# Prompt attention: values with high and low halves side by side, scores three units ahead, more homes for the shares

## What is computed

```python
s_c = einsum('bqghd,bcgd->bghqc', q, kc) * ATTN_SCALE          # compressed keys
p_c = masked_softmax(s_c, c_end[None, :] <= q_pos[:, None])
o_c = einsum('bghqc,bcgd->bqghd', p_c, vc)
s_s = einsum('bqghd,bgqkd->bghqk', q, k_sel) * ATTN_SCALE      # selected blocks: all blocks up to the query here
p_s = masked_softmax(s_s, (s_pos <= q_pos[...]))
o_s = einsum('bghqk,bgqkd->bqghd', p_s, v_sel)
s_w = einsum('bqghd,bwgd->bghqw', q, kw) * ATTN_SCALE          # the window
p_w = masked_softmax(s_w, ...)
o_w = einsum('bghqw,bwgd->bqghd', p_w, vw)
return g[..., 0:1] * o_c + g[..., 1:2] * o_s + g[..., 2:3] * o_w
```

## Time and profile before

| | |
|---|---|
| median of 3 runs | 1760.28 us (1758.5 to 1761.78) |
| the profiled execution | 1756.2 us, span of the trace 1754.6 us |
| mean granted TensorE clock | 0.959 |
| PE, weight loads, DVE, ACT, POOL busy over the span | 93%, 90%, 57%, 41%, 17% |
| prompt attention in the trace | about 186 to 385 us |

### The profile page before, as it was taken

The page is one execution under the profiler, slowest core; times in us unless marked ns, Lnnn a source line. Parts: engine busy times, 40 slices in busy tenths (PEclk is TensorE's granted clock), DMA queues, the critical chain, the costliest instruction groups (busy, mean ns, idle before and its releaser), DMA issues. The chain is left out here.

```text
span 1754.6 us, 31439 instructions
## 1 busy us (share of the span) xinstructions
PE 1630.3 (93%) x12602; PEld 1585.8 (90%) x12602; DVE 998.3 (57%) x1551; ACT 716.6 (41%) x1308; POOL 303.0 (17%) x758
## 2 busy tenths in 40 slices
PE   8998898987998999999998998799899999999986
PEld 8997777866998999999998998799899999999985
DVE  3344476764786435535557595758753454355562
ACT  4444475862444324313334346434442342233341
POOL 4610242440032102102200000001320121021000
PEclk9999699997999999999999999899899999999998
DMA  7744000033212222222231222131222222222211
GB/s 259 134 137 150 1 1 1 1 116 127 74 60 86 89 79 95 86 85 85 86 104 58 90 74 84 54 117 61 73 85 91 78 97 85 85 85 99 81 61 64
DMA packets 39947, 148.01 MB, mean 84 GB/s; under 512 B 6305, under 2 KB 6321, under 8 KB 39361
## 3 DMA queue, kind: packets, MB, share of 16 engines
q1 hardware_dynamic: 33264, 121.26, 21.3%
q0 software_dynamic: 6544, 24.81, 4.2%
HBM read 140.57 MB, written 9.10 MB: 85 GB/s over the span
## 5 line engine op out<-in xcount | busy, mean ns | idle before, releaser
L1805 PE MATMUL PS<-XH,HI 128*128 128x272 f32 (+1 forms) x1936 | 412.4, 295 | 40.7 <-DVE XL L1089 14.1
L1805 PE MATMUL PS<-XH,LO 128*128 128x272 f32 (+1 forms) x1936 | 405.5, 291 | 0.0
L1805 PE MATMUL PS<-XL,HI 128*128 128x272 f32 (+1 forms) x1936 | 404.9, 291 | 0.0
L1805 PEld LDWEIGHTS PS<-XH,HI 128*128 128x128 f32 x1936 | 311.3, 192 | 44.7 <-DVE LO L448 23.4
L442 ACT ACTIVATE HI<-RAW 128x1024 fp32r<-128x1024 f32 x223 | 235.4, 1057 | 283.0 <-PE PS L1805 259.0
L1805 PE MATMUL PS<-GH,HI 128*128 128x272 f32 (+1 forms) x1504 | 320.1, 295 | 23.2 <-DVE LO L448 8.3
L448 DVE TENSOR_TENSOR LO<-RAW,HI 128x1024 fp32r<-128x1024 f32 x223 | 272.3, 1222 | 102.3 <-ACT HI L442 97.0
L1805 PE MATMUL PS<-GH,LO 128*128 128x272 f32 (+1 forms) x1504 | 315.0, 291 | 0.0
L1805 PE MATMUL PS<-GL,HI 128*128 128x272 f32 (+1 forms) x1504 | 314.2, 290 | 0.0
L1805 PEld LDWEIGHTS PS<-XL,HI 128*128 128x128 f32 x1936 | 309.9, 191 | 0.1
L1805 PEld LDWEIGHTS PS<-XH,LO 128*128 128x128 f32 x1936 | 307.9, 191 | 0.0
(11 more groups left out here) (359 smaller groups left out, 1962.6 us busy)
## 6 DMA issues: line engine op xcount, KB each, us to landing
RAW<-in_w_stream SPq DMA_DIRECT2D x223, 512.0 KB, 3.3
ARENA<-in_cache_cmp POOLq DMA_DIRECT2D x32, 128.0 KB, 3.0
out_win_old<-in_win_copy POOLq DMA_DIRECT2D x1, 4064.0 KB, 19.2
X<-in_x SPq DMA_DIRECT2D x4, 544.0 KB, 7.1
X<-in_x POOLq DMA_DIRECT2D x1, 2176.0 KB, 9.2
out_y<-X POOLq DMA_DIRECT2D x1, 2176.0 KB, 6.9
ARENA<-in_cache_sel POOLq DMA_DIRECT2D x16, 128.0 KB, 2.9
ARENA<-in_cache_win POOLq DMA_DIRECT2D x4, 512.0 KB, 5.3
```

The source lines that it names most:

```text
L1805: ins = mm(PS[0:rows, b + h, 0:width], w[:, 0:rows], cols(x, x0 + n, h), start=first, stop=last)
```

## The change

It has four parts.

1. **Values in two passes.** The values' high and low halves of one head group now stand side by side in one weight block `VHL` of 128 columns. One pass with the high shares and one with the low shares give, in one half of the PSUM rows, high values by shares, and in the other half low values by shares. The third pass is gone, for the values and for the compressed values. The output of a group is now in two halves that must be added.
2. **The output in two steps.** ACT copies the half with the low values into SBUF (`out_low_part`), DVE adds the other half (`out_sum`); one unit later ACT makes the high part of the sum (`out_hi`) and DVE the low part (`out_lo`), both from SBUF. PE's waits for the output bank are on `os_ready`, the addition, instead of `ot_lo`.
3. **Three units ahead.** Scores, maximum, exponentials and reciprocal are done for u+3 instead of u+2. The order within a loop turn stays. Three units are done ahead of the loop.
4. **More homes for the shares.** Instead of u % 2 in `P4`, a unit has a home: u % 4 for the first 32 units; by parity for units 32 to 39; from 40 on, the same two for the first two units of a group and two others for the last two. Exponentials wait for the transposes of the unit that was last in the home.

The arena is laid out anew for this, and the copy of the values into `VHL` before the stage is in pieces of 64 columns and waits for the write of the rows they overlay.

```diff
+        VHL = over("VHL", ARENA_AT, at_kt4 + 1024, 2048)
+        V84 = VHL.rearrange("p (b y d) -> p b y d", b=8, y=4)
...
+        VH8, VL8 = V84[:, :, 0:4:3, :], V84[:, :, 1:3, :]
...
+        def home(u):
+
+            if u < 32:
+                return u % 4
+            return u % 2 if u < 40 or u % 4 < 2 else 2 + u % 4
+
+        def before_in_home(u):
+
+            return max([x for x in range(u) if home(x) == home(u)], default=None)
...
-        def sums_of(n):
-
-            gg = group(n)[2]
-            return PS[64 * gg:64 * gg + 64, 6 + n % 2, :].rearrange("p (j t) -> p j t", j=4)
+        def sums_of(n, x):
+
+            row = 64 * (group(n)[2] ^ x)
+            return PS[row:row + 64, 6 + n % 2, :].rearrange("p (j t) -> p j t", j=4)
+
+        def merged(n):
+
+            return heads_of(OSUM, n)
...
-                    s.activation(VH.rearrange("p (h c) -> p h c", h=2), PS[:, 6:8, :], ACT.Copy).then_inc(tr_took, 1)
+                    act.wait_ge(kv_out, 32)
+                    s.activation(VH8, PS[:, 6:8, :].rearrange("p h (b g d) -> p (h b) g d", d=HD, g=2), ACT.Copy).then_inc(tr_took, 1)
...
-                if u >= 2:
-                    act.wait_ge(pt_done, blocks_done(u - 2))
+                if before_in_home(u) is not None:
+                    act.wait_ge(pt_done, blocks_done(before_in_home(u)))
...
+            def out_low_part(n):
+                act.wait_ge(pv_done, n + 1)
+                s.activation(merged(n), sums_of(n, 1), ACT.Copy).then_inc(op_took, 1)
+
             def out_hi(n):
-                act.wait_ge(pv_done, n + 1)
-                s.activation(heads_of(XH3, n), sums_of(n), ACT.Copy).then_inc(ot_hi, 1)
+                act.wait_ge(os_ready, n + 1)
+                s.activation(heads_of(XH3, n), merged(n), ACT.Copy).then_inc(ot_hi, 1)
...
             exps(1)
+            exps(2)
             for u in range(64):
                 n = u // 4
                 if u % 4 == 0 and n >= 2:
+                    out_low_part(n - 2)
+                if u % 4 == 1 and n >= 2:
                     out_hi(n - 2)
...
-                if u < 62:
-                    exps(u + 2)
+                if u < 61:
+                    exps(u + 3)
...
+            def out_sum(n):
+                dve.wait_ge(op_took, n + 1)
+                v.tensor_tensor(merged(n), sums_of(n, 0), merged(n), ALU.add).then_inc(os_ready, 1)
+
             def out_lo(n):
                 dve.wait_ge(ot_hi, n + 1)
-                sub_lo(heads_of(XL3, n), sums_of(n), heads_of(XH3, n), ot_lo)
+                sub_lo(heads_of(XL3, n), merged(n), heads_of(XH3, n), ot_lo)
...
             for u in range(64):
                 n = u // 4
                 if u % 4 == 0 and n >= 2:
+                    out_sum(n - 2)
+                if u % 4 == 1 and n >= 2:
                     out_lo(n - 2)
-                if u < 62:
-                    neg_max(u + 2)
+                if u < 61:
+                    neg_max(u + 3)
...
-                if u < 62:
-                    one_over_sum(u + 2)
+                if u < 61:
+                    one_over_sum(u + 3)
...
                 if n >= 2:
-                    pe.wait_ge(ot_lo, n - 1)
+                    pe.wait_ge(os_ready, n - 1)
...
-                    for m, (v0, pc) in enumerate(((0, hi), (256, hi), (0, lo))):
-                        mm(at[:, :, e, :], VCZ[:, v0 + P * e:v0 + P * e + P],
+                    v0 = P * (2 * e + gg)
+                    for m, pc in enumerate((hi, lo)):
+                        mm(at[:, :, e, :], VCZ[:, v0:v0 + P],
...
-                    vs = slice(r * SEQ + kt * P, r * SEQ + kt * P + P)
-                    for m, (vv, pt) in enumerate(((VH, PTSH[n % 2]), (VL, PTSH[n % 2]), (VH, PTSL[n % 2]))):
-                        ins = mm(at, vv[:, vs], pt[:, r, kt, :], start=False, stop=x == len(blocks) - 1 and m == 2)
+                    v0 = P * (2 * (4 * r + kt) + gg)
+                    for m, pt in enumerate((PTSH[n % 2], PTSL[n % 2])):
+                        ins = mm(at, VHL[:, v0:v0 + P], pt[:, r, kt, :], start=False, stop=x == len(blocks) - 1 and m == 1)
...
             for u in range(64):
                 n = u // 4
-                if u < 62:
-                    scores(u + 2)
+                if u < 61:
+                    scores(u + 3)
...
-            pe.wait_ge(ot_lo, 16)
+            pe.wait_ge(os_ready, 16)
             other_scores(1)
```

More of the change, by code:

```diff
@@ L190, in build, with shares_at @@
         KEPT = [[CACHE[:, 0:4096], CACHE[:, 4096:8192]], CACHE1]
+        def shares_at(name, base, col, step):
+            return [nc.alloc_sbuf_tensor_at(f"{name}{r}", [P, 512], F32, offset=base + 4 * (col + step * r))[:, :] for r in range(2)]
+        PB4 = PB.rearrange("p (u r k) -> p u r k", u=2, r=2)
+        P_OF = [[PB4[:, e, r, :] for r in range(2)] for e in range(2)]
+        P_OF += [shares_at("PQ0", RING_AT, 4608, 1024), shares_at("PQ1", RING_AT, 6656, 1024)]
+        P_OF += [shares_at("PQ2", RING_AT, 1536, 2048), shares_at("PQ3", X_AT, 1536, 2048)]
         def kept(hb, r):
@@ L594, in _ @@
                 for r in range(2):
-                    pr = P4[:, u % 2, r, 0:w]
-                    c = 160 + 2 * (u % 2) + r
+                    pr = P_OF[home(u)][r][:, 0:w]
+                    c = 160 + 2 * (u % 4) + r
                     g0 = 48 * i + 3 * (2 * j + gg) + 1 + r
@@ L794, in exps @@
                 act.wait_ge(negmax_ready, u + 1)
-                if u >= 2:
-                    act.wait_ge(pt_done, blocks_done(u - 2))
+                if before_in_home(u) is not None:
+                    act.wait_ge(pt_done, blocks_done(before_in_home(u)))
                 for r in range(2):
                     c = 2 * (u % 2) + r
-                    ins = s.activation(P4[:, u % 2, r, 0:w], scores_of(u, r), ACT.Exp,
-                                       bias=SMALL[:, 16 + c:17 + c], accum_out=SMALL[:, 64 + c:65 + c])
+                    at = 64 + 2 * (u % 4) + r
+                    ins = s.activation(P_OF[home(u)][r][:, 0:w], scores_of(u, r), ACT.Exp,
+                                       bias=SMALL[:, 16 + c:17 + c], accum_out=SMALL[:, at:at + 1])
                     if r == 0:
@@ L829, in _ @@
                     cmp_hi_part(CMP_TRANS_AT[u])
-                if u < 62:
-                    exps(u + 2)
+                if u < 61:
+                    exps(u + 3)
                 if u in CMP_MASK_AT:
                     cmp_exp(CMP_MASK_AT[u])
+            out_low_part(14)
             out_hi(14)
+            out_low_part(15)
             out_hi(15)
@@ L1219, in one_over_sum @@
                 dve.wait_ge(p_ready, u + 1)
-                v.reciprocal(SMALL[:, 160 + 2 * (u % 2):162 + 2 * (u % 2)],
-                             SMALL[:, 64 + 2 * (u % 2):66 + 2 * (u % 2)]).then_inc(c_ready, 1)
+                at = 2 * (u % 4)
+                v.reciprocal(SMALL[:, 160 + at:162 + at], SMALL[:, 64 + at:66 + at]).then_inc(c_ready, 1)
             def cmp_mask(c):
@@ L1272, in _ @@
             one_over_sum(1)
+            neg_max(2)
+            one_over_sum(2)
             for u in range(64):
@@ L1289, in _ @@
                     cmp_scale(CMP_SCALE_AT[u])
+            out_sum(14)
             out_lo(14)
+            out_sum(15)
             out_lo(15)
@@ L1901, in trans @@
                         at = (x * kts + kt) * P
-                        ins = tr(PS[:, 4 + m % 2, at:at + P], P4[:, u % 2, rr, kt * P:(kt + 1) * P], IDENT[:, :])
+                        ins = tr(PS[:, 4 + m % 2, at:at + P], P_OF[home(u)][rr][:, kt * P:(kt + 1) * P], IDENT[:, :])
                 return ins
@@ L1927, in cmp_values @@
                 if n >= 2:
-                    pe.wait_ge(ot_lo, n - 1)
+                    pe.wait_ge(os_ready, n - 1)
                 if n in (6, 7):
                     pe.wait_ge(sc_masked, n - 3)
-                jq = group(n)[1] // 4
+                jq, gg = group(n)[1] // 4, group(n)[2]
                 at = PS[:, 6 + n % 2, :].rearrange("p (b e t) -> p b e t", b=2, e=2)
@@ L2023, in _ @@
             cmp_scores(1)
+            scores(2)
             for u in range(64):
                 n = u // 4
-                if u < 62:
-                    scores(u + 2)
+                if u < 61:
+                    scores(u + 3)
                 for m, r in blocks_of(u):
```

27 lines of the change are left out of this document (13 added, 14 removed).

## The result

The changed kernel takes 1791.2 us in the median of four runs (1787.9 to 1794.4); the kernel before takes 1760.0 beside it. The ratio is 1.0177, 95% interval 1.0149 to 1.0204. The forecast was 1774, its range ended at 1789. Slower was right, by about twice as much as forecast: +31.2 us instead of +13.9. One of the ten runs of the kernel with both repairs further down, 1834.3 us at a granted clock of 0.82, was in a slow state of the chip and is left out: its median is 1762.8 without that run and 1764.0, as later expectations quote it, with it.

The account below looks back on a forecast made before the run. The prediction held that a serial chain through DVE and ACT bounds prompt attention, PE only level with it. Terms 13.7 + 7.1 - 4.2 - 4.2 + 1.5 = +13.9 us on the 1760.3 median gave 1774.2, range 1758 to 1789.

Parts of the forecast that it names:

- serial chain through DVE and ACT: Prompt attention: maximum, exponentials, reciprocal, next maximum run one after another, 2.8 us a step at 512 keys; PE only level.
- The Trainium skill's rule: Attention stage: relieve the busiest engine, PE by weight loads, so the passes gain most of 22 us; near 1741.
- The second output step: Between exponentials, 13 of 14 groups get a second ACT copy and DVE operation holding the chain, 1.05 us each: +13.7.
- PE lighter: Groups 2 to 5 and 8 onward: DVE's waits for late scores and late sums go, -4.2 us.
- Home wait: Units 35 to 41: exponentials wait for transposes two units back, as only two homes exist; +7.1 us, bounds 0 and 10.
- Compressed scores and head: Unit 25's wait for compressed scores mostly covered, -2.9; third unit's exponentials earlier in the head, -1.3; together -4.2 us.
- The end: After the last exponentials: one more unit to transpose +1.6, value blocks -1.4, second output step +1.3; together +1.5 us.
- The range's lower end: Whole kernel: 1758 us, taking the home wait at 0 and the output step cheaper by 0.5 than its row.
- the clock rival: Attention stage: PE's gaps lower its clock; one pair of groups at half clock +8, so 1782, two pairs 1790; chance 0.12.
- The sign that I gave for being wrong: Attention stage: the prediction counts as wrong if the stage's granted clock falls below 0.9.

Follow-up runs that it names:

- the kernel with both repairs: Changed kernel with four homes for shares up to unit 41 and DVE's two output operations moved behind the subtractions: 1762.8 us, ratio 1.0024.
- the run with PE's old load: Changed kernel with a third matmul of zero weights per value block, so PE does as many columns as before the change: 1791.9 us, ratio 1.0184.

## Why the prediction came out as it did

*What bounds the kernel before* was read rightly: PE level with a serial chain through DVE and ACT. Moving the output step in it gave nothing and made DVE wait for PE 20 times instead of 6, and taking the chain out of the repaired changed kernel gave 13 us. The Trainium skill's rule (Perfetto Trace Analysis, Identifying the Most-Contended Engine: relieve the engine of highest occupancy) would have given 1741. The measured time is 50 us above that. PE's weight loads were busy for 78% and 88% in the earlier trace rows, yet the two passes brought nothing in the changed kernel, nearly 8 us with the outputs out of the chain and two units ahead, and 12.2 us with the reciprocal late as well: the rule named a bound that comes into force only as the waits in front of it go.

*The second output step, +13.7*: right in place and mechanism, too small. It measures 1.32 us per group in the pair at full clock (2.64 for two), so 17 us for the prediction's 13 groups; the changed kernel with two ahead lost 16.9. I had between 1.0 and 1.3 and took 1.05 because PE, lighter, would give some of it back. It doesn't: with PE's old load the pair takes 22.1 us, as with the new one (22.0). The wait for ACT's copy (0.45) and the addition (0.69) make the step.

*PE lighter, -4.2*: this step failed. DVE's waits for late scores did shrink, 6.1 to 3.8 us, but the run with PE's old load costs only 0.7. Where steps have grown by an output step or by a wait, PE has slack already. The prediction took this gain at the old pace of the chain and its costs at the new one.

*Home wait, +7.1 (0 to 10)*: place and cause right, size too small. Six of the seven waits are at units 36 to 41, as named; the seventh, 2.9 us at unit 34, I had taken as hidden at 1.25. Measured 9.4 by the changed kernel with more homes, 11.7 in the kernel with three ahead alone, where PE's transposes stand behind three passes. What I left out is the clock: it was granted 0.84 over groups 9 and 10, and PE was busy 5.3 us longer for the same matmuls.

*Compressed scores and head, -4.2 (0 to -6)*: this step failed too, its sign was wrong. The wait at unit 25 went, as forecast (under 0.5 us). At unit 29 it grew from 2.06 to 5.79 us, with the 32 matmuls at half clock. Groups 7 and 8 take 4.9 us more, of which two output steps at 1.32 explain 2.6, and the stretch to the end of group 2 is 1.5 longer, with one output step in it. Unit 29 had only the words "at unit 29 less" and no term. What brings the lower clock there stays open: it came in every kept trace but that of the kernel before, and moving either the distance or the output step was enough.

*The end, +1.5 (0 to 3)*: 3.9 us between the last reciprocal and the sampled tokens' transposes. No run separates its parts.

*Two sums* of the prediction don't come out as written. The range's lower end with the home wait at 0 and 13 output steps cheaper by 0.5 is 1760.6, not 1758. And twice PE's 16.9 us in a pair at the lower level is 34, not 31, so the clock rival's price would be +11 a pair instead of +8. Neither moves the forecast of 1774.

*The clock* was a rival at 0.12 and +8. The sign that I gave for being wrong, a granted clock of the stage under 0.9, came: from 222 us to the stage's end 0.98 before, 0.86 after. The Trainium skill (TensorE: Matmul & The Clock Gate, HAM oscillation) held that repeated gaps bring the lower level back; the trace agrees (0.86, and 0.50 for whole stretches such as 290 to 306 us), and I had weighed against it gaps of up to 0.9 us, while PE waits up to 3.5 us for DVE's subtractions in the changed kernel. Its price is in the other terms already (5.3 us of PE's time in groups 9 and 10, 3.2 us in the compressed scores), so it can't be added to them; what it costs by itself no run shows, because no run changed the clock without changing the waits.

Against the medians: 16.9 (passes and output steps) + 11.7 (homes) + 4.1 (distance) = 32.7 for 31.2 measured, with part of the 4.1 also in the 16.9, about unit 29. The forecast's 13.9 missed it by too small an output step (3.5), too small a home wait (2 to 5), and two gains of 4.2 that didn't exist.

## What to carry to other kernels

An operation that depends on nothing urgent belongs behind the work that the other engines wait for, in the queue's own idle: one move of two operations in DVE's order gave back 21.9 us of 31. In the kernel before, where PE had no slack, the same move gave nothing. Relieve first what the waits name; the two passes were worth nothing that can be told in the changed kernel and 12.2 us once its other waits were gone. And price gains at the new pace, not at the old: a slack that a cost of the same change opens has already eaten them.

## What the hardware showed that I hadn't expected

Giving PE more to do didn't bring the clock back. The changed kernel's mean granted clock was 0.944 to 0.950; with the third pass of zero weights put back it was 0.950 to 0.952, and with the passes left out but outputs moved, all homes and a late reciprocal 0.954 to 0.957. The waits alone aren't all of it: with the outputs moved it was 0.949 to 0.952, though 21.9 us of waiting were gone.

The lower level stayed for long in one place. In the changed kernel it held from 290 us to the end of the small matmuls at 306 us, with PE busy for 6.1 of the first 9.6 us and without a pause in the rest: 6.68 us for 32 small matmuls. After 6.2 us in which PE was busy for 3.0 they ran at 2.4 GHz, 3.5 us, in the kernel before. That is one execution, and not a secure one: with only the output step moved, nearly the same stretch ahead of them (1.00, PE busy for 2.4 of 4.3 us) was followed by a fall to the lower level in their midst.
